# Chunk inverse by doubling: mask after the product on VectorE instead of before it on GpSimd

## The reference

```
C = GDN_CHUNK                      # 64
A = jnp.where(strict, jnp.einsum('...ik,...jk->...ij', kb, k) * L, 0.0)
Tm = A + jnp.eye(C, dtype=A.dtype)
sol = lax.linalg.triangular_solve(Tm, rhs, left_side=True, lower=True, unit_diagonal=True)
```

## Time and profile before

| | |
|---|---|
| median of 3 runs | 2909.74 us (2908.99 to 2910.17) |
| span of the profiled execution | 2907.5 us |
| TensorE matmul busy | 2767.4 us, 95% |
| TensorE weight load busy | 2202.0 us, 76% |
| VectorE busy | 1481.1 us, 51% |
| ScalarE busy | 1068.4 us, 37% |
| GpSimd busy | 573.2 us, 20% |
| GpSimd masks (L1644) | 162 instructions, 118.6 us, mean 737 ns |
| mean granted TensorE clock | 0.988 |

### The profile page before, as it was taken

The page is one execution under the profiler, slowest core; times in us unless marked ns, Lnnn a source line. Parts: engine busy times, 40 slices in busy tenths (PEclk is TensorE's granted clock), DMA queues, the critical chain, the costliest instruction groups (busy, mean ns, idle before and its releaser), DMA issues. The chain is left out here.

```text
span 2907.5 us, 58953 instructions
## 1 busy us (share of the span) xinstructions
PE 2767.4 (95%) x22859; PEld 2202.0 (76%) x22859; DVE 1481.1 (51%) x3089; ACT 1068.4 (37%) x3237; POOL 573.2 (20%) x737
## 2 busy tenths in 40 slices
PE   7999999999999999999999898899998999999998
PEld 4778768898766667898766777768895678867887
DVE  7554447642244327753542455337726864447651
ACT  2234334422432224422655444324412134324431
POOL 0013210063213210064100223110160003210044
PEclk9999999999999999999999999999999999999999
DMA  5420124444333224443433004533342330123442
GB/s 154 154 74 6 37 74 142 132 129 117 84 108 98 65 78 131 131 132 121 130 104 94 6 6 130 154 121 130 124 133 73 123 102 6 25 68 122 131 134 79
DMA packets 356657, 287.83 MB, mean 99 GB/s; under 512 B 74700, under 2 KB 352765, under 8 KB 355997
## 3 DMA queue, kind: packets, MB, share of 16 engines
q1 hardware_dynamic: 337456, 267.03, 29.9%
q10 hardware_dynamic: 14828, 14.93, 1.6%
q0 software_dynamic: 4096, 2.11, 0.4%
HBM read 263.29 MB, written 20.73 MB: 98 GB/s over the span
## 5 line engine op out<-in xcount | busy, mean ns | idle before, releaser
L359 PE MATMUL bank<-h,weights 128*128 128x320 f32 (+2 forms) x3152 | 788.6, 408 | 8.1 <-ACT h L444 8.1
L359 PEld LDWEIGHTS bank<-h,weights 128*128 128x128 f32 (+1 forms) x3152 | 567.9, 189 | 217.3 <-issue 17.1
L359 PE MATMUL bank<-arena,weights 128*128 128x320 f32 (+5 forms) x3088 | 664.7, 374 | 10.8 <-DVE arena L1404 6.6
L359 PE MATMUL bank<-arena 128*128 128x160 f32 (+7 forms) x5034 | 640.8, 291 | 11.8 <-DVE arena L2744 5.1
L359 PEld LDWEIGHTS bank<-arena,weights 128*128 128x128 f32 (+2 forms) x3088 | 505.0, 188 | 153.7 <-issue 23.1
L359 PEld LDWEIGHTS bank<-arena 128*128 128x128 f32 (+2 forms) x5034 | 544.5, 172 | 36.2 <-issue 14.1
L1644 POOL TENSOR_TENSOR arena<-arena,consts 128x256 f32<-128x256 f32 x162 | 118.6, 737 | 774.9 <-DVE arena L1971 453.6
L568 POOL TENSOR_TENSOR arena<-weights 128x512 f32<-128x512 f32 (+1 forms) x48 | 59.7, 1243 | 724.2 <-DMA weights<-ffn_w_down 628.3
L359 PE MATMUL bank<-h,arena 64*64 64x64 f32 (+3 forms) x3000 | 178.3, 234 | 11.6 <-POOL arena L1644 9.2
L359 PEld LDWEIGHTS bank<-h,arena 64*64 64x64 f32 (+1 forms) x3000 | 153.7, 144 | 18.9 <-POOL arena L1644 12.9
L891 DVE SCALAR_TENSOR_TENSOR arena<-arena,params 128x336 f32<-128x336 f32 x176 | 106.3, 604 | 67.5 <-ACT arena L751 58.8
(11 more groups left out here) (373 smaller groups left out, 3748.8 us busy)
## 6 DMA issues: line engine op xcount, KB each, us to landing
weights<-ffn_w_up SPq DMA_DIRECT2D x88, 1024.0 KB, 5.1
weights<-ffn_w_down SPq DMA_DIRECT2D x32, 1024.0 KB, 5.2
weights<-rw_wrkv SPq DMA_DIRECT2D x24, 1024.0 KB, 5.3
weights<-gdn_w_in SPq DMA_DIRECT2D x24, 1024.0 KB, 5.4
arena<-cache_mla_latent SPq DMA_DIRECT2D x108, 128.0 KB, 2.3
weights<-ffn_w_down SPq DMA_DIRECT2D x16, 768.0 KB, 4.9
weights<-rw_wo SPq DMA_DIRECT2D x8, 1024.0 KB, 5.2
weights<-gdn_wo SPq DMA_DIRECT2D x8, 1024.0 KB, 5.8
```

The source lines that it names most:

```text
L359: return pe.matmul(out, lhsT, rhs, start=first, stop=last, skip_group_check=True)
```

## The change

The mask moves behind the product. From level 1 on TensorE multiplies the unmasked `am` with `inv`. Because `inv` is block diagonal at that point, the wanted block of the product is the same, and the other blocks are thrown away when the product leaves its bank: VectorE multiplies it by `low1` to `low5` into `p` (`dve_level_product`). ScalarE's copy of `p` goes, GpSimd keeps level 0 alone, and TensorE's product no longer waits for a mask from level 1 on. Step `p` is now VectorE's, and its semaphore is shared with VectorE's other chunk steps.

```diff
-        cols[f"hlev{lev}"] = (row // (2 * w) == col // (2 * w)) & ((row // w) % 2 == 0) & ((col // w) % 2 == 1)
+        if lev == 0:
+            cols["hlev0"] = (row // 2 == col // 2) & (row % 2 == 0) & (col % 2 == 1)
+        else:
+            cols[f"low{lev}"] = (row // (2 * w) == col // (2 * w)) & ((row // w) % 2 == 1) & ((col // w) % 2 == 0)
...
-        def pool_level(pool, l, n, lev):
+        def pool_first_level(pool, l, n):
             un = unit_of(n, l)
             pool.wait_ge(*at("am", (l, n, 3)))
-            if lev:
-                pool.wait_ge(*at("pmm", (l, n, lev - 1)))
-                if lev == 1:
-                    pool.wait_ge(*at("inv", (l, n, 0)))
...
-                for lev in levels(2 * g):
-                    for n in group(g):
-                        pool_level(pool, l, n, lev)
+                for n in group(g):
+                    pool_first_level(pool, l, n)
...
         def pe_level_product(pe, l, n, lev):
-            pe.wait_ge(*at("off", (l, n, lev)))
             if lev:
                 pe.wait_ge(*at("inv", (l, n, lev - 1)))
+            else:
+                pe.wait_ge(*at("off", (l, n, 0)))
...
-                    out, off = ps[hs, el * 64:el * 64 + 64], un["off"][hs, el, :]
+                    out, off = ps[hs, el * 64:el * 64 + 64], (un["am"][hs, el, 0:64] if lev else un["off"][hs, el, :])
...
-            act.wait_ge(*at("pmm", (l, n, lev)))
-            act.activation(un["p"], of(("p", l, n, lev))[:, 0:256].rearrange("p (a b) -> p a b", a=4), ACT.Copy).then_inc(*to("p", (l, n, lev)))
...
+        def dve_level_product(dve, l, n, lev):
+            un = unit_of(n, l)
+            dve.wait_ge(*at("pmm", (l, n, lev)))
+            dve.tensor_tensor(un["p"], of(("p", l, n, lev))[:, 0:256].rearrange("p (a b) -> p a b", a=4),
+                              const(f"low{lev}").unsqueeze(1).broadcast_to([P, 4, 64]), ALU.mult).then_inc(*to("p", (l, n, lev)))
...
-                    if lev == 0:
-                        for n in group(g):
-                            dve_level(dve, l, n, lev)
+                    for n in group(g):
+                        (dve_level_product if lev else dve_level)(dve, l, n, lev)
```

More of the change, by code:

```diff
@@ L134 @@
     "decays": "decay_prev decay decay_inv decay_end",
-    "rwkv_chunk_copies": "tv p invt rhs sa mg pstate",
+    "rwkv_chunk_copies": "tv invt rhs sa mg pstate",
     "rwkv_sample_copies": "sout",
@@ L153 @@
     "group_norm": "bonus_v y_centered y1 y2 y3 y_gated",
-    "rwkv_chunk_sums": "am inv y state m0 z sam m_new",
+    "rwkv_chunk_sums": "am p inv y state m0 z sam m_new",
     "ffn_taps": "tap1 conv xp_zero",
@@ L1635, in group_steps @@
             return steps[:count], steps[count:]
-        def pool_level(pool, l, n, lev):
+        def pool_first_level(pool, l, n):
             un = unit_of(n, l)
             pool.wait_ge(*at("am", (l, n, 3)))
-            if lev:
-                pool.wait_ge(*at("pmm", (l, n, lev - 1)))
-                if lev == 1:
-                    pool.wait_ge(*at("inv", (l, n, 0)))
-            pool.tensor_tensor(un["off"], un["am"][:, :, 0:64], const(f"hlev{lev}").unsqueeze(1).broadcast_to([P, 4, 64]),
-                               ALU.mult).then_inc(*to("off", (l, n, lev)))
+            pool.tensor_tensor(un["off"], un["am"][:, :, 0:64], const("hlev0").unsqueeze(1).broadcast_to([P, 4, 64]),
+                               ALU.mult).then_inc(*to("off", (l, n, 0)))
         def pool_rwkv_chunks(pool, l):
```

## The result

The changed kernel took 2889.4 us (median of 6 runs, 2885.2 to 2895.3) against 2907.1 for the kernel before (6 runs, 2901.5 to 2910.2): ratio 0.9941, interval 0.9930 to 0.9953, 17.6 us less. The forecast was 2899.0, 10.7 less than the 2909.7 that the kernel before had in its first three runs, with 2891 as its lower end. The sign and the main mechanism were right, the size was not. The six runs of before lie 2.7 us lower than the first three; that shift alone is more than the 1.6 us by which the result lies under the lower end.

What follows compares the result with a forecast made beforehand. The prediction took TensorE, busy 95% of the span, as the bound, losing time at hand-overs. Terms 10.7 - 0.6 - 2.4 + 1.5 = 9.2 us, plus 1.5 for the clock, turned 2909.7 into 2899.0 us; range 2891 to 2907.

Steps and rivals of the forecast that it cites:

- Level-1 wait: Level-1 products no longer wait for GpSimd's mask: 5.0 us gained in rwkv layers, 5.2 plus 0.5 in gated-delta, 10.7 together.
- Copy on VectorE: 132 copies move from ScalarE to VectorE; the next update waits slightly longer for some: 0.6 us lost, at most 2.6.
- Gate: Layer 2, groups 2 and 3: copies queue behind the output gate, delaying the level-2 update 1.2 us each: 2.4 us lost.
- What GpSimd's queue does instead: Rwkv layers, groups 1 and 2: head masks run earlier, no longer beside VectorE's state updates: net 1.5 us gained, bounds 0 and 2.
- sister wait: Layer 3, group 2: TensorE's gap at a state update beside the head masks, read as 0.31 us.
- Clock: Layer 2's chunk stage: less idle time spares one of about four stretches at 1.2 GHz, 1.5 us gained.
- the first: Rival: all four low-clock stretches spared, 5.2 us instead of 1.5, about 2895, or 2892 with a high level-1 term; chance 0.15.
- The second: Rival: level 1 then waits on ScalarE's right-hand-side copy and L1983, regaining half; 1.3 to 5 us, about 2906; chance 0.16.
- The third: Rival: each copy stands behind another VectorE instruction, 0.42 us for each of 66 update pairs; slower, 2925; chance 0.07.
- The fourth: Rival: nothing measurable changes, since masks were already hidden at levels 2 to 5; 2909.7; chance 0.06.

Runs made afterwards that it cites:

- wait_layers03: Changed kernel with GpSimd's level-1 mask, and TensorE's wait for it, put back in layers 0 and 3 alone: 2892.5 us, ratio 0.9960 to before.
- first_gate_behind: Changed kernel with only the first output gate of layer 2's groups 2 and 3 moved behind the level-2 masked copies: 2887.0 us, ratio 0.9936 to before.
- before_again: Kernel before, no edit, profiled a second time: one execution, 2907.6 us.
- masks_beside: Changed kernel with the 132 GpSimd mask instructions put back at levels 1 to 5, nobody waiting for them: 2894.9 us, ratio 0.9974 to before.
- level1_only: Kernel before with the change at level 1 alone; levels 2 to 5 keep GpSimd's mask and ScalarE's copy: 2893.3 us, ratio 0.9959 to before.
- levels2up_only: Kernel before with the change at levels 2 to 5 alone; level 1 still masks on GpSimd and waits: 2903.3 us, ratio 0.9997 to before.
- after_again: Changed kernel, no edit, profiled a second time: one execution, 2889.4 us.
- heads_late: Changed kernel with GpSimd's head masks held until the level-4 product of groups 1 and 2: 2890.0 us, ratio 0.9953 to before.

## Why the size was wrong

By the prediction's steps, with before and after as means of two profiles each for layers 0 and 3 (152.8 and 153.7 us became 147.1 and 147.2, a gain of 5.7 and 6.5):

- **Level-1 wait, forecast 10.7.** Right. In layers 0 and 3 the gaps at level 1 shrank by 2.7 us each, 5.3 against 5.0. The spread was off: group 0 gave 0.37 in layer 0 and 0.17 in layer 3, where nothing was expected, and group 2 gave 0.34 instead of 0.84, as L1980 ran beside the head masks. `wait_layers03` puts 5.2 us back at these matmuls. In layer 2, 4 x 1.4 + 0.5 = 6.1 against 5.7.
- **Copy on VectorE, forecast -0.6.** Right in kind: TensorE waited 1.2 us for L1993, five times.
- **Gate, forecast -2.4.** Right: 1.05 us each, 2.1; `first_gate_behind` regained 2.2.
- **Unforeseen, -1.0:** level 0's mask beside L2752 in layer 2's group 0. I had looked at what GpSimd's shorter queue moves in the rwkv layers and not in layer 2.
- **Failed step: "What GpSimd's queue does instead", forecast +1.5.** The step priced the old place of the head masks at two waits of 0.66 and two of 0.31 us. At all four places both state updates were slowed, to 1.10 and 0.94 us from 0.28. On the mean of two profiles each, TensorE's matmuls there (1984 to 2000, 2872 to 2888, 18202 to 18218, 19090 to 19106) came back 3.5 us sooner. The sister wait of 0.31 us was read where a stop of 0.42 us just ahead of it covered part of it; before_again has no stop there and waits 0.66 us. Layer 0, group 2, shows the same, first before, then before_again at the same matmuls:

```profile
263.18 0.83 PEld L359 LDWEIGHTS bank<-arena,h 64*64 64x64 f32 x25 [0.55 <-issue]
...
264.48 0.22 PEld L359 LDWEIGHTS bank<-post_scaled,arena 64*64 64x64 f32 x4 [0.24 <-issue]
```

```profile
263.69 0.22 PEld L359 LDWEIGHTS bank<-post_scaled,arena 64*64 64x64 f32 x4 [0.66 <-ACT post_scaled L1907]
```

  Another 1.0 us is small delays at other places in the two layers, which I had put at nothing: 4.5 in all. `masks_beside` lost 2.3 + 2.2 = 4.5 us too, 3.4 of them behind the state updates, 1.0 at other places and 0.6 in the stops of the next item; 0.4 came back at level 1. So most of the term is the head masks' place and little of it the level masks by themselves: the gaps behind the state updates stayed in `level1_only`, which keeps the place, and went in `levels2up_only`, which frees it.
- **Left out: stops that the profile puts down to "issue".** At matmuls some 125 apart in layers 0 and 3 TensorE stops for 0 to 1.2 us. Their excess over the shortest seen is 2.8 and 3.0 us in before, 2.3 and 3.8 in before_again, 1.8 and 1.9 in the changed kernel, 1.1 and 2.0 in after_again: on the mean 2.6 us less after the change. Part of it belongs to the execution (up to 0.8 us between profiles of one kernel), and `levels2up_only` had only 1.4 and 1.2 with the level-1 wait in place. What sets them stays open; 2.6 us of the gain may not be the change's own.
- **Clock, forecast one stretch, 1.5.** In groups 1 to 3 of layer 2 the compared profiles show three fewer (13.6 us at 1.2 GHz), worth 117.2 - 111.8 = 5.4 us by before_again. But before_again shows none in the same code, so the difference of two profiles overstates it. Over all profiles, groups 1 to 3 of layer 2 had 3, 0, 3, 1 and 1 stretches in the five kernels or repeats whose level-1 product waits for a mask there, and none in the other twelve. By this count the wait makes them likely and not certain; why a stretch comes in one execution and not in the next is not shown, and behind 13440 two kernels without the wait have one. Between matmuls 10860 and 13950 the low time was 30.7 and 13.7 us before and 17.1 twice after, on the mean 5.1 less, at the rate above (5.4 us for 13.6) 2.0 us.

The sum: 5.7 + 6.5 = 12.2 for layers 0 and 3, and 6.1 - 2.1 - 1.0 + 2.0 = 5.0 for layer 2, where 217.0 us became 211.7 between matmuls 10860 and 13950. Together 17.2. The medians differ by 17.6 and the spans of the two pairs of profiles by 18.6 on the mean; the rest of the program, where two profiles of before alone differ by 3.3 us, leaves the difference open. Of the 6.9 us that the forecast lacked, 3.0 are GpSimd beside VectorE, 2.6 the issue stops, 0.5 the clock; the rest are the small differences above and 0.4 outside these stages.

The rivals: the first (the clock stays up, 2895 or 2892) happened in part, and its all-or-nothing form was wrong. The Trainium skill's TensorE: Matmul & The Clock Gate (A second HAM failure mode: psum-queue depth-cycling), by which small idle gaps between groups of matmuls make the clock oscillate, agrees with 8 stretches in 5 profiles against none in 12, but not with before_again, which had the gaps and not the stretches. The second (another wait takes over) held for one product in group 2 of layers 0 and 3 alone. The third (VectorE's queue bounds) was right at the gate only. The fourth is ruled out by the result: the interval, 0.9930 to 0.9953, leaves out 1.

## What to carry to other kernels

Price the removal of a helper's work in two parts: the wait that it ended, which the waits view gives (11.4 us measured, 10.7 forecast), and the neighbours that it slowed (4.5 us, 1.5 forecast), which wait rows name only in part and under other engines' names. Look for the second among instructions of one form whose longest is over twice the median, and price it by TensorE's gap at each of their places, in two profiles: a stop just ahead can hide a wait. When an engine's queue gets shorter, follow all that is behind it to its new place in every stage: the same edit freed the state updates at four places and hit L1980 and L2752. Where two profiles differ by a low-clock stretch, take a second profile of the same kernel before it becomes a term.

## What the runs showed of the hardware

- VectorE instructions with all inputs in SBUF took 0.3 to 0.8 us more beside GpSimd: 8 columns 0.16 to 0.69, 64 columns 0.28 to 1.10, L1980 0.42 to 0.92, the gate's two 0.75 to 1.07 and 0.69 to 1.10. The loss doesn't follow their own length. Two short ones ended just behind the GpSimd instruction that they met: the copy of 8 columns at 1619.17, the mask at 1619.14; the first state update in `masks_beside` at 228.47, the first head mask at 228.40. The prediction said "both inputs in SBUF"; the copy has one and was slowed too. The 132 masked copies out of a bank took 0.41 to 0.43 us, beside GpSimd as well. The Trainium skill's GPSIMD Engine Reference (Specifications) puts contention with GpSimd on VectorE instructions with two SBUF inputs or in a 2-port mode. The traces agree for those with two; no run shows in which mode the copy runs.
- TensorE's stops put down to "issue" lie at the same matmuls in every kernel, about 125 apart in this part. The profile's queue q8, of the kind "instruction", moved 184 packets in all, one per 22859 / 184 = 124 matmuls:

```profile
q8 instruction: 184, 3.01, 0.4%
```

  That points to the supply of instructions, but no run here varied it, and why a stop is 0 in one kernel and 1.2 us in another was not tried.
- With the clock up, groups 1 to 3 of layer 2 repeat to 0.02 us in the four profiles whose code is the same there (changed 111.29, after_again 111.27, `heads_late` 111.28, `wait_layers03` 111.28). The rest of the program, outside layers 0 and 3 and matmuls 10860 to 13950, varied between 2377.2 and 2386.9 us with the same code; part of it is a 10.2 us stretch at 1.2 GHz some 815 us from the start that some profiles have and some don't.
